# One block for the output product and two feed-forwards, a late norm root, and tensors on 128-byte lines

## The chip, the cores and the metric

One Trainium2 chip, one core. The time is device microseconds (us) of one execution. Engines: PE (TensorE: the matmuls), PEld (its weight loads), DVE (VectorE), ACT (ScalarE), POOL (GpSimd), SP (SyncE, here only the issuer of DMAs).

## The reference, cut to what matters

Two transformer blocks over 512 tokens of width 1024, in float32. The change touches the end of the first and the start of the second:

```
x = x + merged @ w_out                                   # output product
h = rms_norm(x, norm_ffn_g);   g, u = split(h @ w_ffn_in)   # 1024 -> 2 x 2816
x = x + (silu(g) * u) @ w_ffn_out                        # first feed-forward, 2816 -> 1024
h = rms_norm(x, ffn1_pre_g);   g, u = split(h @ ffn1_w_gu)
y = (silu(g) * u) @ ffn1_w_down                          # second feed-forward
x = x + 0.5 * rms_norm(y, ffn1_post_g)                   # post norm
rms_norm(x, g) = x * rsqrt(mean(x * x) + eps) * g
```

The factor rsqrt(...) belongs to a token, so it can be applied before the product with the weights or after it. The rest (attention branches, a state-space branch, a third feed-forward) is not edited.

## The kernel before

Features lie on the 128 partitions, tokens along the free dimension: x is 8 chunks of [128, 512]. Every product is one stream of weight units. A unit holds up to 8 chunks of 128x128 weights (512 KB), loaded by SP into one of two raw slots; ACT rounds it to w_hi (split_hi, line 155), DVE takes w_lo = w_raw - w_hi (split_lo, line 166). Both start when PE has used the unit two places earlier. The moving operand is held as hi and lo too, and each chunk is three matmuls of 512 columns: hi*hi, hi*lo, lo*hi (lines 193 to 195). A tile of 8 chunks is 24 matmuls into one of two banks, acc[0] and acc[1]. The stream runs on through the stages: the last two units of a stage fetch and split the first two of the next.

Each stage is a block of its own: five instruction streams, joined at its end. Four of them matter here.

- `down_stage` for the output product: 8 tiles over `merged`. After each tile DVE adds acc to x (line 649), ACT squares x (line 629), DVE adds that to the sum of squares ssq (line 656).
- `feed_forward_stage`, twice. It opens with `Norm`: PE multiplies ssq by ones (line 326), which gives every partition the sum; ACT takes Ln and Exp of it (lines 336, 338) for rstd; then for each of 8 chunks DVE forms normed = x * gain * rstd (line 357), ACT rounds it to h_hi (line 343), and h_lo = normed - h_hi goes to POOL for even chunks and DVE for odd ones (line 347). Then 22 rounds of a gate tile and an up tile: ACT takes Silu of acc[0], DVE multiplies by acc[1] (line 538), hid is split. Then 8 down tiles of 22 chunks (units of 8, 8 and 6).
- `post_norm_stage` after the second: the same sum over ones, from ssq.

The order of work is the order written in each engine's stream; semaphores hold the counts.

Where the tensors lie. The compiled program of before starts each tensor at the next multiple of 32 bytes in its partition. The shared ones come first: x_res at 16,512 bytes (129 x 128), h_hi at 32,896 (257 x 128), then h_lo, ssq, w_raw, w_hi, w_lo, small (283 columns, 1,132 bytes), ones, ident at 93,952 (734 x 128), all on multiples of 128. Then eps, subln_eps and log_half take one column, that is 32 bytes, each. So whatever a stage allocates starts at 94,560, 96 bytes past a multiple of 128; as their sizes are multiples of 128, hid_hi, hid_lo, merged, y_gla, y_swa, y_da, y_ssd_s, y_xa and mem_h all sit 96 bytes off.

Of the kernel before, what the change touches and what calls it, by code (L numbers as in the profile page):

```python
# [19 lines left out]
F32 = mybir.dt.float32  # L20
F32R = mybir.dt.float32r
# [20 lines left out]
NT = S // P  # L42
MASKED = -1e30
NUM_SEMAPHORES = 256

def small_layout():

    cols, at = {}, 0  # L50
    for name, n in (
        ("norm_mix_g", KC), ("norm_ffn_g", KC), ("ffn1_pre_g_2", KC), ("ffn1_post_g_2", KC),
        ("mix_pre_g_2", KC), ("mix_post_g_2", KC), ("xa_pre_g_2", KC), ("xa_post_g_2", KC),
        ("mem_norm_g_2", KC), ("ffn2_pre_g_2", KC), ("ffn2_post_g_2", KC),
        ("gla_gate_bias_fwd", 4), ("gla_gate_bias_bwd", 4), ("gla_out_norm_g", 2),
        ("swa_q_norm_g", 1), ("swa_k_norm_g", 1), ("b_gate_2", 2 * KC), ("da_subln_g_2", 1),
        ("ssd_conv_w_2", 4 * 24), ("ssd_conv_b_2", 24), ("ssd_norm_g_2", 16),
        ("swa_sinks", 8), ("ssd_D_2", 16), ("ssd_dt_bias_2", 1), ("ssd_A_log_2", 1),
        ("lam_q1", 1), ("lam_k1", 1), ("lam_q2", 1), ("lam_k2", 1),
    ):  # L60
        cols[name] = (at, n)
        at += n
    return cols, at


SMALL, SMALL_N = small_layout()
# [6 lines left out]
def alloc(nc, ctx, c):  # L73

    def sb(name, shape, dt=F32):
        return ctx.enter_context(nc.sbuf_tensor(name, shape, dt))

    c.x = sb("x_res", [P, KC, S])
    c.h_hi = sb("h_hi", [P, KC, S], F32R)
    c.h_lo = sb("h_lo", [P, KC, S], F32R)  # L80
    c.ssq = sb("ssq", [P, S])
    c.raw = sb("w_raw", [P, 2, KC * P])
    c.w_hi = sb("w_hi", [P, 2, KC * P], F32R)
    c.w_lo = sb("w_lo", [P, 2, KC * P], F32R)
# [226 lines left out]
class Norm:  # L311
# [54 lines left out]
    def ready(self, pe, k):  # L366

        pe.wait_ge(self.lo_done[k % 2], k // 2 + 1)
# [90 lines left out]
def feed_forward_stage(c, s_up, s_down, following, gain, in_bank, parts, y, add):  # L459
# [106 lines left out]
    enter(down)  # L566
    c.unit += s_down.rounds * s_down.n
    c.tile += s_down.rounds * s_down.tiles


@stage
# [1705 lines left out]
def build_program(nc, a, out):  # L2277
# [214 lines left out]
```

## Time and profile before

| what | value |
|---|---|
| median of 3 runs | 2982.87 us (2980.98 to 2983.17) |
| profiled execution, first to last instruction (span) | 2979.1 us |
| PE busy | 2715.2 us, 91% of the span |
| DVE, ACT, POOL busy | 42%, 35%, 5% |
| granted TensorE clock, mean | 0.954 |
| output product, the two feed-forwards and their norms | 584.7 to 1387.4 us of the span |

The median lies 3.8 us over the span; the profile has no other time of its own. PE is the busiest engine. The groups further down say where it stands still.

### The profile page before, as it was taken

The numbers are of one execution on the slowest core, as the hardware profiler recorded it, in microseconds if no ns is written. First come the engines' busy times: TensorE is split into PE (matmuls) and PEld (weight loads), VectorE is DVE, ScalarE is ACT, GpSimd is POOL, SyncE is SP. The second block draws the span as 40 slices with busy tenths as digits, with TensorE's granted clock in tenths as the row PEclk, the third lists the DMA queues.
The fourth block names the chain that finished last, engine by engine and source line by source line (L and its number), as shares of the span: only waits on it lengthen the run. The fifth ranks groups of instructions, "written<-read, shape, count | busy, mean of one in ns | idle before, by whom it ended". The sixth has DMA issues, their size and how long they took to land. (4 is left out here: it accounts for less than half of the span.)

```text
span 2979.1 us, 34509 instructions
## 1 busy us (share of the span) xinstructions
PE 2715.2 (91%) x12052; PEld 2163.3 (73%) x12052; DVE 1257.7 (42%) x1709; ACT 1051.7 (35%) x1661; POOL 152.5 (5%) x95
## 2 busy tenths in 40 slices
PE   4998999989999899997899799988899798799997
PEld 3876777768888688885667677766677587588885
DVE  5343543343333433334334235666633633533333
ACT  4443544232222332223344334444422433333221
POOL 0000000000000000001000000111201400100000
PEclk8999999999999999998889899999999899899998
DMA  2121111222223222232111123232222131122332
GB/s 88 64 70 67 64 63 64 85 77 98 99 91 95 78 95 99 94 93 71 45 51 53 53 78 110 97 99 92 71 87 96 64 105 66 55 94 99 99 90 79
DMA packets 69448, 240.86 MB, mean 81 GB/s; under 512 B 7968, under 2 KB 8992, under 8 KB 69264
## 3 DMA queue, kind: packets, MB, share of 16 engines
q1 hardware_dynamic: 69392, 240.14, 24.4%
q8 instruction: 32, 0.52, 0.1%
q14 instruction: 24, 0.20, 0.0%
HBM read 237.94 MB, written 2.16 MB: 81 GB/s over the span
## 5 line engine op out<-in xcount | busy, mean ns | idle before, releaser
L166 DVE TENSOR_TENSOR w_lo<-w_raw,w_hi 128x1024 fp32r<-128x1024 f32 (+1 forms) x422 | 514.1, 1219 | 1081.8 <-ACT w_hi L155 1081.0
L193 PE MATMUL acc<-h_hi,w_hi 128*128 128x512 f32 x2176 | 876.1, 403 | 58.8 <-POOL h_lo L347 19.1
L194 PE MATMUL acc<-h_lo,w_hi 128*128 128x512 f32 x2176 | 856.1, 393 | 0.0
L195 PE MATMUL acc<-h_hi,w_lo 128*128 128x512 f32 x2176 | 856.0, 393 | 0.0
L155 ACT ACTIVATE w_hi<-w_raw 128x1024 fp32r<-128x1024 f32 (+1 forms) x422 | 441.4, 1046 | 1108.4 <-PE acc L195 1106.0
L193 PEld LDWEIGHTS acc<-h_hi,w_hi 128*128 128x128 f32 x2176 | 414.2, 190 | 164.3 <-issue 69.7
L194 PEld LDWEIGHTS acc<-h_lo,w_hi 128*128 128x128 f32 x2176 | 414.5, 190 | 89.9 <-issue 6.1
L195 PEld LDWEIGHTS acc<-h_hi,w_lo 128*128 128x128 f32 x2176 | 413.8, 190 | 88.9
L193 PE MATMUL acc<-10_hid_hi,w_hi 128*128 128x512 f32 x176 | 69.6, 396 | 0.0
L193 PE MATMUL acc<-12_hid_hi,w_hi 128*128 128x512 f32 x176 | 69.6, 396 | 0.0
L193 PE MATMUL acc<-32_hid_hi,w_hi 128*128 128x512 f32 x176 | 69.6, 396 | 0.0
L194 PE MATMUL acc<-10_hid_lo,w_hi 128*128 128x512 f32 x176 | 69.6, 396 | 0.0
L195 PE MATMUL acc<-10_hid_hi,w_lo 128*128 128x512 f32 x176 | 69.6, 396 | 0.0
L194 PE MATMUL acc<-12_hid_lo,w_hi 128*128 128x512 f32 x176 | 69.6, 396 | 0.0
L195 PE MATMUL acc<-12_hid_hi,w_lo 128*128 128x512 f32 x176 | 69.6, 396 | 0.0
L194 PE MATMUL acc<-32_hid_lo,w_hi 128*128 128x512 f32 x176 | 69.6, 396 | 0.0
L195 PE MATMUL acc<-32_hid_hi,w_lo 128*128 128x512 f32 x176 | 69.6, 396 | 0.0
L193 PE MATMUL acc<-merged_hi,w_hi 128*128 128x512 f32 x128 | 52.3, 409 | 12.1 <-PEq L227 6.3
L1067 DVE CUSTOM_DVE_ANT_0 16_s<-16_score,15_mask 128x128 f32<-128x128 f32 (+3 forms) x64 | 29.2, 489 | 62.2 <-PE 16_score L1053 62.2
L2184 DVE SCALAR_TENSOR_TENSOR 20_m<-20_conv_in,20_taps,20_m 128x512 f32<-128x512 f32 x72 | 54.1, 752 | 2.6
L193 PE MATMUL acc<-y_ssd_s_hi,w_hi 128*128 128x512 f32 x128 | 51.4, 402 | 3.5 <-DVE w_lo L166 3.5
L2270 POOL TENSOR_TENSOR 20_xs<-20_xs,20_moved 128x384 f32<-128x384 f32 x16 | 18.5, 1158 | 682.2 <-DVE 20_xs L2253 681.7
(441 smaller groups left out, 3548.9 us busy)
## 6 DMA issues: line engine op xcount, KB each, us to landing
w_raw<-in_w_gu SPq DMA_DIRECT2D x132, 512.0 KB, 3.2
w_raw<-in_w_down SPq DMA_DIRECT2D x48, 512.0 KB, 3.5
w_raw<-in_w_ssd SPq DMA_DIRECT2D x40, 512.0 KB, 3.2
w_raw<-in_w_swa SPq DMA_DIRECT2D x28, 512.0 KB, 3.2
w_raw<-in_w_gla SPq DMA_DIRECT2D x24, 512.0 KB, 3.3
w_raw<-in_w_da SPq DMA_DIRECT2D x24, 512.0 KB, 3.2
w_raw<-in_w_ssd_out SPq DMA_DIRECT2D x24, 512.0 KB, 3.2
w_raw<-in_w_xa SPq DMA_DIRECT2D x24, 512.0 KB, 3.2
```

Source lines behind the costliest of these rows:

```text
L155: c.nc.scalar.activation(c.w_hi[:, k % 2, 0:chunks * P], c.raw[:, k % 2, 0:chunks * P], ACT.Copy).then_inc(c.hi_done, 1)
L166: c.nc.vector.tensor_tensor(c.w_lo[:, k % 2, 0:chunks * P], c.raw[:, k % 2, 0:chunks * P], c.w_hi[:, k % 2, 0:chunks * P].bitcast(F32), AL ...
L193: pe.matmul(out, hi, x_hi[:, j, 0:cols], start=first, stop=False)
L194: pe.matmul(out, hi, x_lo[:, j, 0:cols], start=False, stop=False)
L195: mm = pe.matmul(out, lo, x_hi[:, j, 0:cols], start=False, stop=final)
L1067: dve.tensor_tensor_reduce(to, self.score[j % 2][:, 0:count], self.bias(n), self.scale, floor, ALU.add, ALU.max, self.top[:, par, j:j + 1] ...
L2184: ins = dve.scalar_tensor_tensor(out, u[:, n % 2, k:k + S], tap(k), out, ALU.mult, ALU.add)
L2270: pool.tensor_tensor(y[:, j, P:], y[:, j, P:], moved[:, j % 2, P:], ALU.add).then_inc(q["joined"], 1)
```

## The change

1. `trunk_stage` replaces `down_stage` (output product) and both `feed_forward_stage` calls by one block, so nothing joins the engines between them. The rounds of the output and down products are written out; those of gate and up stay a loop (its first round's PE work is written out).
2. `LateRoot` replaces `Norm`. When a chunk of x is done, ACT writes h_hi = x * gain and DVE h_lo = x * gain - h_hi at once, without the root. PE multiplies ssq by ones after the first gate tile, into a bank of its own; ACT takes the root then, with the same Ln and Exp. DVE multiplies each gate and each up tile by rstd as it leaves acc.
3. ssq is summed by POOL (`gather`), no longer by DVE, from two buffers of squares.
4. `small` is padded to 288 columns, and the three constants share one tensor of 32 columns (128 bytes), so everything allocated after them starts on a multiple of 128.
5. `merged` is read in the new block after its allocation has been closed; hid_lo, written only after the output product, takes its place.

The diff, cut:

```diff
+LINE = 32
...
-    return cols, at
+    return cols, -(-at // LINE) * LINE
...
-    c.eps = sb("eps", [P, 1])
-    c.subln_eps = sb("subln_eps", [P, 1])
-    c.log_half = sb("log_half", [P, 1])
+    constants = sb("constants", [P, LINE])
+    c.eps, c.subln_eps, c.log_half = (constants[:, n:n + 1] for n in range(3))
...
+class LateRoot:
...
+    def split_hi(self, act, t, n, gain):
+        act.wait_ge(self.x_done, n + t + 1)
+        act.activation(self.c.h_hi[:, t, :], self.c.x[:, t, :], ACT.Copy,
+                       scale=self.gain(gain, t)).then_inc(self.hi_done, 1)
...
+    def split_lo(self, dve, t, n, gain):
+        dve.wait_ge(self.hi_done, n + t + 1)
+        at = t
+        dve.scalar_tensor_tensor(self.c.h_lo[:, at, :], self.c.x[:, at, :], self.gain(gain, t),
+                                 self.c.h_hi[:, at, :].bitcast(F32), ALU.mult, ALU.subtract).then_inc(self.lo_done, 1)
+
+    def gather(self, pool, t, par, n):
+        pool.wait_ge(self.squared, n + t + 1)
+        pool.wait_ge(self.summed, (n // KC + 1) + n + t)
+        pool.tensor_tensor(self.c.ssq[:], self.c.ssq[:], self.sq[:, par, :], ALU.add).then_inc(self.summed, 1)
+
+    def mean_square(self, pe, norm):
+        pe.wait_ge(self.summed, (norm + 1) * (KC + 1))
+        pe.matmul(self.mean[:], self.c.ones[:], self.c.ssq[:], start=True, stop=True).then_inc(self.total, 1)
+
+    def root(self, act, norm):
+        act.preload_act_table_set(EXP_LN_SET)
+        act.wait_ge(self.total, norm + 1)
+        act.activation(self.rstd[:], self.mean[:], ACT.Ln, scale=1.0 / D, bias=self.c.eps[:, 0:1]).then_inc(self.log_done, 1)
+        act.wait_ge(self.log_done, norm + 1)
+        act.activation(self.rstd[:], self.rstd[:], ACT.Exp, scale=-0.5).then_inc(self.rstd_done, 1)
...
+        @block.tensor
...
+            for i in range(KC // 2):
+                out_pair(i)
+            for f in range(2):
+                enter(up_phases[f])
+                multiply_tile(c, pe, 0, 0, 0, h, norm=Ready(root.lo_done, KC * f))
+                root.mean_square(pe, f)
+                multiply_tile(c, pe, 0, 1, 1, h)
+                with pe.Fori(1, FFC) as i:
+                    gate_up(i)
+                enter(down_phases[f])
+                for i in range(KC // 2):
+                    down_pair(i, f)
...
+        @block.scalar
+        def _(act):
+            def pair(i, n, units, gain, y):
+                for t in range(2):
+                    for k in range(t * units, (t + 1) * units):
+                        split_hi(c, act, i, k)
+                    if gain is not None:
+                        root.split_hi(act, 2 * i + t, KC * n, gain)
+                    root.square(act, y, 2 * i + t, t, KC * n)
+
+            def gate_up(i, f):
+                split_hi(c, act, i, 0)
+                act.wait_ge(gate_done, FFC * f + i + 1)
+                act.activation(silu[:], gate[:], ACT.Silu).then_inc(silu_done, 1)
+                split_hi(c, act, i, 1)
+                act.wait_ge(hid_done, FFC * f + i + 1)
+                act.activation(hid_hi[:, bass.ds(i, 1), :], hid[:], ACT.Copy).then_inc(hid_hi_done, 1)
...
+                root.root(act, f)
+                act.preload_act_table(ACT.Silu)
+                with act.Fori(0, FFC) as i:
+                    gate_up(i, f)
...
+        @block.vector
...
+            def pair(i, n, units, gain, add):
...
+                    wait_tile(c, dve, i, last)
+                    at = 2 * i + t
+                    if add:
+                        dve.tensor_tensor(c.x[:, at, :], c.x[:, at, :], c.acc[t][:], ALU.add).then_inc(c.acc_free[t], 1)
...
+                    wait_evacuated(c, dve, i, t)
+                    dve.sem_inc(root.x_done, 1)
+                    split_lo(c, dve, i, last)
+                    if gain is not None:
+                        root.split_lo(dve, 2 * i + t, KC * n, gain)
+
+            def gate_up(i, f):
+                n = FFC * f + i
+                wait_tile(c, dve, i, 0)
+                dve.tensor_tensor(gate[:], c.acc[0][:], root.rstd[:], ALU.mult).then_inc(gate_done, 1)
+                dve.wait_ge(gate_done, n + 1)
+                dve.sem_inc(c.acc_free[0], 1)
+                split_lo(c, dve, i, 0)
+                wait_tile(c, dve, i, 1)
+                dve.tensor_tensor(up[:], c.acc[1][:], root.rstd[:], ALU.mult).then_inc(c.acc_free[1], 1)
+                dve.wait_ge(silu_done, n + 1)
+                wait_evacuated(c, dve, i, 1)
+                dve.tensor_tensor(hid[:], silu[:], up[:], ALU.mult).then_inc(hid_done, 1)
+                split_lo(c, dve, i, 1)
+                dve.wait_ge(hid_hi_done, n + 1)
+                dve.tensor_tensor(hid_lo[:, bass.ds(i, 1), :], hid[:], hid_hi[:, bass.ds(i, 1), :].bitcast(F32),
+                                  ALU.subtract).then_inc(hid_lo_done, 1)
...
-            down_stage(c, s_out, s_gu1, *merged, [(0, KC)], c.x, True)
-        feed_forward_stage(c, s_gu1, s_dn1, s_gu2, "norm_ffn_g", False, DOWN, c.x, True)
...
-            feed_forward_stage(c, s_gu2, s_dn2, s_da, "ffn1_pre_g_2", False, DOWN, y, False)
+            trunk_stage(c, merged, (s_out, (s_gu1, s_gu2), (s_dn1, s_dn2)), s_da,
+                        ("norm_ffn_g", "ffn1_pre_g_2"), DOWN, y)
```

## Rows read from the trace of the kernel before

**Rows 1.** The page: part 1, and the high-part split of part 5.

```profile
...
PE 2715.2 (91%) x12052; PEld 2163.3 (73%) x12052; DVE 1257.7 (42%) x1709; ACT 1051.7 (35%) x1661; POOL 152.5 (5%) x95
...
L155 ACT ACTIVATE w_hi<-w_raw 128x1024 fp32r<-128x1024 f32 (+1 forms) x422 | 441.4, 1046 | 1108.4 <-PE acc L195 1106.0
```

**Rows 2.** Busy time by stretch (us, PE, PEld, DVE, ACT, POOL, clock, DMA share, GB/s).

```profile
...
631.00:650.00 19.00, 9.82 (x27) 6.25 (x27) 13.86 (x15) 10.62 (x14) 6.82 (x4) 0.73 0.15 55
650.00:884.00 234.00, 234.00 (x1034) 193.74 (x1033) 79.82 (x85) 69.57 (x86) 0.00 (x0) 1.00 0.29 96
884.00:1007.00 123.00, 123.00 (x529) 99.01 (x527) 38.09 (x41) 28.18 (x32) 0.00 (x0) 1.00 0.30 91
1007.00:1027.00 20.00, 10.34 (x28) 5.97 (x27) 13.86 (x15) 10.57 (x14) 6.82 (x4) 0.74 0.14 52
```

**Rows 3.** Timeline of the first seam (start us, us taken, ...).

```profile
...
630.66 0.40 PE L195 MATMUL acc<-merged_hi,w_lo 128*128 128x512 f32 x1
...
633.33 0.68 DVE L656 TENSOR_TENSOR ssq<-ssq,9_sq 128x512 f32<-128x512 f32 x1
...
634.33 1.10 PE L326 MATMUL acc<-ssq,ones 128*128 128x512 f32 x2 [3.27 <-PEq L227]
...
636.31 0.63 ACT L338 ACTIVATE 11_rstd<-11_rstd 128x512 f32<-128x512 f32 x1
...
640.32 0.76 PE L193 MATMUL acc<-h_hi,w_hi 128*128 128x512 f32 x1 [4.89 <-POOL h_lo L347]
...
640.88 0.63 PE L194 MATMUL acc<-h_lo,w_hi 128*128 128x512 f32 x1
...
641.31 0.63 PE L195 MATMUL acc<-h_hi,w_lo 128*128 128x512 f32 x1
...
650.09 0.40 PE L193 MATMUL acc<-h_hi,w_hi 128*128 128x512 f32 x1
```

**Rows 4.** Timeline of the second seam, first to second feed-forward.

```profile
...
1007.00 0.40 PE L195 MATMUL acc<-10_hid_hi,w_lo 128*128 128x512 f32 x1
...
1010.62 1.28 ACT L333 ACT_TABLE_LOAD   x1 [1.56 <-PEq L469]
...
1010.66 1.91 PE L326 MATMUL acc<-ssq,ones 128*128 128x512 f32 x2 [3.27 <-PEq L469]
...
1012.62 0.69 ACT L336 ACTIVATE 13_rstd<-acc,eps 128x512 f32<-128x512 f32 x1 [0.71 <-PE acc L326]
...
1027.11 0.40 PE L193 MATMUL acc<-h_hi,w_hi 128*128 128x512 f32 x1
```

**Rows 5.** Timeline of PE, where h gives way to hid as moving operand.

```profile
...
881.08 0.39 PE L195 MATMUL acc<-h_hi,w_lo 128*128 128x512 f32 x1
...
884.03 0.40 PE L193 MATMUL acc<-10_hid_hi,w_hi 128*128 128x512 f32 x1
...
886.83 0.40 PE L193 MATMUL acc<-10_hid_hi,w_hi 128*128 128x512 f32 x1
```

**Rows 6.** Groups of PE instructions by operand (busy us, mean ns).

```profile
...
L193 PE MATMUL acc<-h_hi,w_hi 128*128 128x512 f32 x2176 | 876.1, 403 | 58.8 <-POOL h_lo L347 19.1 <-PEq L227 19.0 <-PEq L732 13.2
...
L193 PE MATMUL acc<-10_hid_hi,w_hi 128*128 128x512 f32 x176 | 69.6, 396 | 0.0
...
L193 PE MATMUL acc<-merged_hi,w_hi 128*128 128x512 f32 x128 | 52.3, 409 | 12.1 <-PEq L227 6.3 <-DVE merged_lo L387 5.8
...
L193 PE MATMUL acc<-mem_h_hi,w_hi 128*128 128x256 f32 x128 | 39.1, 306 | 9.6 <-DVE w_lo L166 7.3 <-ACT 29_rstd L336 2.3
...
L193 PE MATMUL acc<-y_swa_hi,w_hi 128*128 128x512 f32 x64 | 25.3, 396 | 0.0
```

**Rows 7.** The low-part split among the groups by form, 640 to 1007 us.

```profile
...
L166 DVE TENSOR_TENSOR w_lo<-w_raw,w_hi 128x1024 fp32r<-128x1024 f32 x59 | 72.4, 1227 | 178.5 <-ACT w_hi L155 178.5
```

**Rows 8.** Timeline of the first seam, POOL beside DVE.

```profile
...
638.47 3.39 POOL L347 TENSOR_TENSOR h_lo<-11_normed,h_hi 128x512 fp32r<-128x512 f32 x2 [606.69 <-ACT h_hi L343]
639.09 1.64 DVE L347 TENSOR_TENSOR h_lo<-11_normed,h_hi 128x512 fp32r<-128x512 f32 x1
```

More of the change, by code:

```diff
@@ L568, in feed_forward_stage, with __init__, gain, clear @@
     c.tile += s_down.rounds * s_down.tiles
+class LateRoot:
+    def __init__(self, c, ctx):
+        sb, ps, sem = local(c, ctx)
+        self.c = c
+        self.sq, self.rstd, self.mean = sb("sq", [P, 2, S]), sb("rstd", [P, S]), ps("mean")
+        self.x_done, self.squared, self.summed = sem("x_done"), sem("squared"), sem("summed")
+        self.hi_done, self.lo_done = sem("h_hi"), sem("h_lo")
+        self.total, self.log_done, self.rstd_done = sem("total"), sem("log"), sem("rstd")
+    def gain(self, name, t):
+        return vec(self.c, name, t)
+    def clear(self, dve):
+        dve.memset(self.c.ssq[:], 0.0).then_inc(self.summed, 1)
+    def split_hi(self, act, t, n, gain):
+        act.wait_ge(self.x_done, n + t + 1)
+        act.activation(self.c.h_hi[:, t, :], self.c.x[:, t, :], ACT.Copy,
+                       scale=self.gain(gain, t)).then_inc(self.hi_done, 1)
+    def square(self, act, y, t, par, n):
+        act.wait_ge(self.x_done, n + t + 1)
+        act.wait_ge(self.summed, (n // KC + 1) + n + t - 1)
+        act.activation(self.sq[:, par, :], y[:, t, :], ACT.Square).then_inc(self.squared, 1)
+    def split_lo(self, dve, t, n, gain):
[16 more added lines that the diff above has]
+        act.activation(self.rstd[:], self.rstd[:], ACT.Exp, scale=-0.5).then_inc(self.rstd_done, 1)
@@ new lines, with __init__, ready, trunk_stage @@
+class Ready:
+    def __init__(self, done, first):
+        self.done, self.first = done, first
+    def ready(self, pe, k):
+        pe.wait_ge(self.done, self.first + k + 1)
+def trunk_stage(c, merged, streams, following, gains, parts, y):
+    s_out, ups, downs = streams
+    order = [s_out, ups[0], downs[0], ups[1], downs[1]]
+    phases, unit, tile = [], c.unit, c.tile
+    for n, s in enumerate(order):
+        phases.append((s, order[n + 1] if n + 1 < len(order) else following, unit, tile))
+        unit, tile = unit + s.rounds * s.n, tile + s.rounds * s.tiles
+    out_phase, up_phases, down_phases = phases[0], phases[1::2], phases[2::2]
+    def enter(phase):
+        c.stream, c.following, c.unit, c.tile = phase
+    with ExitStack() as ctx:
+        sb, ps, sem = local(c, ctx)
+        root = LateRoot(c, ctx)
+        gate, silu, up, hid = sb("gate", [P, S]), sb("silu", [P, S]), sb("up", [P, S]), sb("hid", [P, S])
+        hid_hi, hid_lo = sb("hid_hi", [P, FFC, S], F32R), sb("hid_lo", [P, FFC, S], F32R)
+        gate_done, silu_done, up_done, hid_done, hid_hi_done, hid_lo_done = (
+            sem("gate"), sem("silu"), sem("up"), sem("hid"), sem("hid_hi"), sem("hid_lo"))
+        sources = [(hid_hi[:, a:b, :], hid_lo[:, a:b, :]) for a, b in parts]
+        per = len(parts)
+        block = ctx.enter_context(c.nc.Block())
+        @block.sync
+        def _(sp):
+            for phase in phases:
+                enter(phase)
+                stream_loads(c, sp, c.stream, c.following)
+        @block.tensor
+        def _(pe):
+            h = [(c.h_hi, c.h_lo)]
+            def out_pair(i):
+                for t in range(2):
+                    multiply_tile(c, pe, i, t, t, [merged])
+            def gate_up(i):
+                multiply_tile(c, pe, i, 0, 0, h)
+                multiply_tile(c, pe, i, 1, 1, h)
+            def down_pair(i, f):
+                for t in range(2):
+                    multiply_tile(c, pe, i, t * per, t, sources, norm=None if t else Ready(hid_lo_done, FFC * f))
+            enter(out_phase)
+            for i in range(KC // 2):
[13 more added lines that the diff above has]
+            def pair(i, n, units, gain, y):
+                for t in range(2):
+                    for k in range(t * units, (t + 1) * units):
[10 more added lines that the diff above has]
+                act.activation(hid_hi[:, bass.ds(i, 1), :], hid[:], ACT.Copy).then_inc(hid_hi_done, 1)
+            enter(out_phase)
+            for i in range(KC // 2):
+                pair(i, 0, 1, gains[0], c.x)
+            for f in range(2):
+                enter(up_phases[f])
+                root.root(act, f)
+                act.preload_act_table(ACT.Silu)
+                with act.Fori(0, FFC) as i:
+                    gate_up(i, f)
+                enter(down_phases[f])
+                for i in range(KC // 2):
+                    pair(i, f + 1, per, gains[1] if f == 0 else None, c.x if f == 0 else y)
+        @block.vector
+        def _(dve):
+            def pair(i, n, units, gain, add):
+                for t in range(2):
+                    last = (t + 1) * units - 1
+                    for k in range(t * units, last):
+                        split_lo(c, dve, i, k)
+                    wait_tile(c, dve, i, last)
+                    at = 2 * i + t
+                    if add:
+                        dve.tensor_tensor(c.x[:, at, :], c.x[:, at, :], c.acc[t][:], ALU.add).then_inc(c.acc_free[t], 1)
+                    else:
+                        dve.tensor_copy(y[:, at, :], c.acc[t][:]).then_inc(c.acc_free[t], 1)
+                    wait_evacuated(c, dve, i, t)
[19 more added lines that the diff above has]
+                                  ALU.subtract).then_inc(hid_lo_done, 1)
+                dve.wait_ge(hid_lo_done, n + 1)
+            root.clear(dve)
+            enter(out_phase)
+            for i in range(KC // 2):
+                pair(i, 0, 1, gains[0], True)
+            for f in range(2):
+                enter(up_phases[f])
+                dve.wait_ge(root.rstd_done, f + 1)
+                with dve.Fori(0, FFC) as i:
+                    gate_up(i, f)
+                enter(down_phases[f])
+                root.clear(dve)
+                for i in range(KC // 2):
+                    pair(i, f + 1, per, gains[1] if f == 0 else None, f == 0)
+        @block.gpsimd
+        def _(pool):
+            for n in range(3):
+                for i in range(KC // 2):
+                    for t in range(2):
+                        root.gather(pool, 2 * i + t, t, KC * n)
+    enter(phases[-1])
+    c.unit, c.tile = unit, tile
```

## The prediction

> **What bounds the kernel now.** I read the page first: PE is busy 91% of the span, DVE 42%, ACT 35% [rows 1]. So a saving counts only where it shortens PE's own work or a stretch in which PE stands still. The chain of waits on the page starts only at 2961 us, so it says nothing of this place; I cut the time into stretches instead [rows 2]. In the gate and up rounds and in the down tiles PE is busy for the whole stretch (234.00 of 234.00 us, 123.00 of 123.00) at full clock. Between them lie two seams of 19 and 20 us in which PE works some 10 us at a granted clock of 0.73 and 0.74. There are thus two quantities: what a seam costs, and what one matmul costs in a full stretch.
>
> The timeline of a seam [rows 3]. The last matmul of the output product starts at 630.66, so the next could start at 630.9. From then on the engines follow each other: the split of the last weights, x, its square, ssq done at 634.01; the block ends; the sum over ones at 634.33; Ln, Exp to 636.94; normed, h_hi, h_lo of chunk 0; the first gate matmul at 640.32. It runs at the lower of the two clock levels (1.2 GHz: 0.43 us from start to start at 640.88), then waits for later chunks. The second tile starts at 650.09.
>
> The time of a full tile [rows 5]. With h as moving operand, 13 starts lie in 884.03 - 881.08 = 2.95 us, 226.8 ns each; a tile of 24 is 5.44 us. With hid, 12 lie in 886.83 - 884.03 = 2.80 us, 233.3 ns each. Clock, weights, shape and accumulator are the same, and the change comes with the first hid matmul.
>
> **The two seams.** Undisturbed, the second gate-side tile would start at 630.9 + 5.44 = 636.33; it starts at 650.09: the first seam costs 13.8 us. The second: 1007.0 + 0.23 + 5.44 = 1012.67 against 1027.11, 14.4 us [rows 4]. Together 28.2 us. The change should leave of each, counting from the end E of the product before it:
>
> - Chunk 7 of h. ACT: 0.2 us of lag, w_hi 1.05, h_hi 0.63, square 0.63 (with a gain as scale, taken as 0.63; the nearest row with a per-partition operand is 0.69), done at E+2.5 [rows 1, 3, 4]. DVE: w_lo 1.23 behind w_hi, then h_lo 0.7, done at E+3.3 [rows 7]. PE wants chunk 7 as the last of eight, at 21 x 0.2267 = E+4.8; chunks 0 to 6 are a tile older. The weights of the first gate unit are split since the tile before. Stall 0. Against it: POOL now runs gather, 1.70 us [rows 8], at the same moment. In the old seam one DVE subtraction beside POOL takes 1.64 us [rows 8] where a DVE instruction of that shape alone takes 0.68 [rows 3]. If gather starts first, h_lo ends at E+5.0: 0.2 us late. Bounds 0 and 0.3 us.
> - The sum over ones goes between two tiles of PE. It is two instructions, 1.91 us in the second seam and 1.10 in the first [rows 3, 4]. Both spans reach to the modelled end of the second one, which lies behind the start of what follows. I take 0.9 us of PE time (half of 1.91 is 0.95), bounds 0.8 and 1.1. ssq for it is ready: square E+2.5, gather to E+4.3, or E+5.0 if it yields to DVE, before E+5.44.
> - The root. Sum done E+6.5, Ln 0.69, Exp 0.63: rstd at E+7.9 [rows 3, 4]. DVE then empties acc[0] by E+8.6. Behind the root in ACT's stream stand the Silu table, 1.28 us [rows 4], and the w_hi split for the third tile, 1.05: E+10.3; w_lo behind it E+11.6. PE wants these weights at 5.44 + 0.9 + 5.44 = E+11.8, and acc[0] then as well. It fits by 0.2 us: this is the tightest place of the change. I allow 0.2 us of stall, bounds 0 and 1.0.
>
> So a seam keeps 0.9 + 0.1 + 0.2 = 1.2 us (bounds 0.8 and 2.4), both 2.4 us. Since PE has no pause there, I expect no stretch at the lower clock level either. Gain 28.2 - 2.4 = 25.8 us.
>
> Against it stands the end of the block. The post norm still waits for ssq. Now: E, then 3.1 us to the end of the last addition by DVE (as in the first seam: 634.01 - 630.9) [rows 3]. Then: 0.2 + 1.05 + 0.63 + 0.1 + gather 1.70 = 3.7 us. It costs 0.6 us (bounds 0, if little of this shows, and 1.7, a whole gather). **Net for the seams: 25.2 us.**
>
> **Work inside the rounds, costed at nothing.** DVE's round grows by two multiplications (0.7 us each) and ACT's Silu reads SBUF. After an up tile at T: up, hid, w_lo: 0.15 + 0.7 + 0.7 + 1.23 = T+2.8, hid_lo T+3.5; PE wants w_lo at T+5.44. After a gate tile: gate 0.7, then w_lo at T+2.4. The cover is 2.6 us in each tile; a round would have to lose that much before PE saw it. DVE per round is 2 x 1.23 + 4 x 0.7 = 5.3 us of 10.9. In the output and down tiles DVE's queue holds w_lo behind a wait for x, as before, and h_lo replaces the ssq addition at the same length. gather may hold DVE back 1.7 us at 24 places; the shortest tile there leaves about 2 us. SP's queue keeps its order and its waits. Rolled loops leave no gap at their ends in a full stretch [rows 2], so writing them out gains nothing.
>
> **The lines.** The front section gives the addresses: h and ssq lie on multiples of 128 bytes, everything stage-local 96 bytes off. Another local operand, y_swa, of other size and place, has hid's mean of 396 ns [rows 6]; those of h and merged, 403 and 409, hold the slow seams too. If the start is the reason, each gives back 6.7 ns. The counts, times three for the three products [rows 6]: hid 3 stages x 3 x 176 = 1584; merged 384, y_ssd_s as many; y_swa and its three likes (y_gla, y_da, y_xa) 4 x 192 = 768. Sum 3120 x 6.67 ns = 20.8 us. They stand in stretches that PE sets, except perhaps half of y_gla's 1.3 us. mem_h has half the columns: 384 x 3.3 ns = 1.3 us, of which I count half. For the other 2,020 or so PE instructions of local operands (12,052 less 3 x 2,176 on h, 3,120 and 384) [rows 1, 6] the bound is 3.3 ns each, 6.7 us; most are short and sit in chains of ACT and DVE, I take 0.3 us. **Sum 21 us**, bounds 0 and 28.8 us. For DVE and ACT I take nothing: no row of theirs differs by more than 0.01 us between shared and local tiles of one shape that I saw, and they do not set these stretches.
>
> What speaks against this part: the Trainium skill (SBUF — State Buffer, Specifications) gives SBUF lines of 16 bytes. 96 is a multiple of 16, so by that page the operands lie well already and this term is 0; the rows show a step of 6.7 ns at the first hid matmul, but not what makes it.
>
> **Sum.** 25.2 + 21 = 46.2 us off the profiled span of 2979.1: 2932.9. The median stands 3.8 us above the span, so 2936.7 us.
>
> **Rivals.**
>
> - B, the lines do nothing: what makes hid slower is something else (its size, its distance from its partner). For it: no row has a local tensor on a line. Against it: y_swa and hid differ in size and place and share the pace, and h keeps its own in every stretch. Then 2982.9 - 25.2 = 2957.7 us. 10%.
> - C, a seam keeps a stall: the third tile's weights (0.2 us of room) or h_lo come 3 us late, because the two table loads or a wait between ACT and DVE take longer than their rows. 2 x 3.2 = 6.4 us more: 2943 us. Against it: each step is a row of the old seam. 9%.
> - D, slower: the clock falls in a block that never pauses. For it: PE has not been without a seam for more than 357 us here (650.09 to 1007.0); now it is some 770. Against it: both full stretches hold 1.00 to their end [rows 2]. At the lower level a matmul takes 0.43 instead of 0.23 us [rows 3, 5], so 46.2 us are given back after 231 matmuls, about 100 us of block at half clock. If the clock stayed low for the last 400 us, 1,750 matmuls x 0.2 us = 350 us more: about 3290 us. 3%.
> - E, a cost that eats all: within 0.2% of before. 1%, no mechanism that I can name.
>
> **How the numbers follow.** A, as worked out, has 77%. With every bound in its favour it is 28.2 - 1.6 = 26.6 us for the seams and 28.8 for the lines: 2928. With the bounds against it: seams 28.2 - 4.8 - 1.7 = 21.7; lines (1056 + 192) x 6.7 ns = 8.3 us in this block and half of the other 12.5, 14.5: 2947. The range of 2928 to 2951 us takes A and C and leaves B, D and E out. A measurement of this kernel tells 0.2%, 6 us, from no change. Faster: A, B, C, 96%. Same: 1%. Slower: D, 3%.
>
> **What would show it.** PE's timeline at the seams: last product matmul to second tile in 6.6 us, two instructions on ssq between the first two tiles, granted clock 1.00 through both. A hid matmul's mean of 389 or 390 ns in place of 396, and merged, y_da and the third feed-forward likewise outside the block. POOL with 24 additions of 1.7 us. The forecast is wrong if hid keeps 396 ns, if PE waits on w_lo before the third tile, or if the clock in the last third of the block is below 1.00.

## The result, and the profile of the changed kernel

| | time, median (range, runs) | span of the profiled execution |
|---|---|---|
| before | 2982.57 us (2980.98 to 2983.17, 4) | 2979.1 us |
| changed | 2934.26 us (2933.12 to 2936.50, 4) | 2934.5 us |

The ratio is 0.9843, 95% interval 0.9826 to 0.9860: 48.3 us less. The forecast was 2936.7 us. In every execution on record the time is 1.8 to 2.1 us above that execution's own span. A second set of runs of the same kernel gave 2932.92 us (2931.86 to 2935.45, 6 runs), ratio 0.9850 [0.9828, 0.9871].

The page of the changed kernel, first the engines and then four groups. They answer to [rows 1, 6, 8].

```profile
PE 2687.7 (92%) x12052; PEld 2161.0 (74%) x12052; DVE 1291.6 (44%) x1765; ACT 1051.4 (36%) x1661; POOL 180.4 (6%) x111
...
L193 PE MATMUL acc<-h_hi,w_hi 128*128 128x512 f32 x2176 | 873.8, 402 | 47.7 <-PEq L227 18.5
...
L193 PE MATMUL acc<-9_hid_hi,w_hi 128*128 128x512 f32 x352 | 136.9, 389 | 0.0
...
L613 POOL TENSOR_TENSOR ssq<-ssq,10_sq 128x512 f32<-128x512 f32 x24 | 42.4, 1766 | 1275.7 <-ACT 10_sq L602 1275.7
...
L751 DVE TENSOR_TENSOR 9_gate<-acc,10_rstd 128x512 f32<-128x512 f32 x44 | 30.4, 691 | 105.8 <-PE acc L195 96.0
```

The number of PE instructions is the same. A hid matmul has a mean of 389 ns where it had 396; y_swa, y_da and the hid of the third feed-forward have 389 too. The mean of merged, 407 ns, still holds matmuls at the lower clock level. POOL has 24 additions of 1.77 us; DVE has the 0.69 us multiplications. DVE's added work doesn't show in PE's.

Busy time by stretch, with the columns of [rows 2]: the end of the output product, the first seam with the first gate and up round, the other rounds, the first down stage, the second seam, the second gate and up rounds, the second down stage.

```profile
595.00:626.00 31.00, 31.00 (x138) 25.70 (x137) 16.93 (x17) 11.99 (x17) 9.99 (x6) 1.00 0.31 99
626.00:645.00 19.00, 19.00 (x83) 15.37 (x82) 8.45 (x11) 10.60 (x13) 1.85 (x1) 1.00 0.28 89
645.00:866.00 221.00, 221.00 (x976) 183.00 (x976) 101.79 (x121) 65.84 (x81) 0.00 (x0) 1.00 0.29 96
866.00:986.00 120.00, 120.00 (x531) 99.34 (x531) 40.23 (x42) 32.33 (x39) 12.42 (x7) 1.00 0.32 95
986.00:1004.00 18.00, 18.00 (x79) 14.56 (x78) 8.00 (x10) 9.66 (x12) 1.85 (x1) 1.00 0.34 115
1004.00:1226.00 222.00, 222.00 (x981) 183.87 (x980) 102.25 (x122) 66.76 (x82) 0.00 (x0) 1.00 0.30 96
1226.00:1346.00 120.00, 120.00 (x531) 99.32 (x529) 34.51 (x35) 28.02 (x32) 12.62 (x7) 1.00 0.32 95
```

PE is busy for the whole of each stretch and the granted clock is 1.00, the 2.4 GHz level, also in the stretches that hold the seams. In [rows 2] a stretch of 19 us around the seam had 9.82 us of PE at 0.73.

The timeline of the first seam, beside which [rows 3] are to be laid:

```profile
626.03 0.39 PE L195 MATMUL acc<-merged_hi,w_lo 128*128 128x512 f32 x1
...
626.26 0.39 PE L193 MATMUL acc<-h_hi,w_hi 128*128 128x512 f32 x1
...
626.46 1.06 ACT L155 ACTIVATE w_hi<-w_raw 128x1024 fp32r<-128x1024 f32 x1 [3.25 <-PE acc L195]
626.46 0.69 DVE L739 TENSOR_TENSOR x_res<-x_res,acc 128x512 f32<-128x512 f32 x1 [1.33 <-PE acc L195]
...
627.42 0.70 ACT L595 ACTIVATE h_hi<-x_res,small 128x512 fp32r<-128x512 f32 x1
627.55 1.23 DVE L166 TENSOR_TENSOR w_lo<-w_raw,w_hi 128x1024 fp32r<-128x1024 f32 x1 [0.41 <-ACT w_hi L155]
...
628.69 0.74 DVE L607 SCALAR_TENSOR_TENSOR h_lo<-x_res,small,h_hi 128x512 fp32r<-128x512 f32 x1
628.73 1.85 POOL L613 TENSOR_TENSOR ssq<-ssq,10_sq 128x512 f32<-128x512 f32 x1 [4.15 <-ACT 10_sq L602]
...
631.70 1.02 PE L617 MATMUL 10_mean<-ssq,ones 128*128 128x512 f32 x2
...
632.16 0.80 PE L193 MATMUL acc<-h_hi,w_hi 128*128 128x512 f32 x1
...
632.76 0.69 ACT L622 ACTIVATE 10_rstd<-10_mean,constants 128x512 f32<-128x512 f32 x1 [2.81 <-PE 10_mean L617]
632.80 0.39 PE L194 MATMUL acc<-h_lo,w_hi 128*128 128x512 f32 x1
...
635.43 1.06 ACT L155 ACTIVATE w_hi<-w_raw 128x1024 fp32r<-128x1024 f32 x1
...
636.52 1.22 DVE L166 TENSOR_TENSOR w_lo<-w_raw,w_hi 128x1024 fp32r<-128x1024 f32 x1 [1.50 <-ACT w_hi L155]
...
638.04 0.39 PE L193 MATMUL acc<-h_hi,w_hi 128*128 128x512 f32 x1
```

The first gate matmul follows the last output matmul after 0.23 us, the ordinary distance. h_lo of chunk 7 is done at 629.43, E+3.2 with E = 626.26, long before PE wants it. The addition by POOL starts 0.04 us after h_lo and doesn't hold it back (h_lo takes 0.74 us, the addition 1.85). Between the tiles stands the sum over ones. The root follows; the third tile's low-part weights are done at 637.74 and its first matmul starts at 638.04. Two tiles of 5.44 us and the seam take 638.04 - 626.26 = 11.78 us: **the seam keeps 0.9 us.** The second seam is the same, 986.20 to 997.98.

The same timeline where h gives way to hid, as in [rows 5]:

```profile
863.80 0.39 PE L193 MATMUL acc<-h_hi,w_hi 128*128 128x512 f32 x1
...
866.52 0.39 PE L193 MATMUL acc<-9_hid_hi,w_hi 128*128 128x512 f32 x1
...
869.24 0.39 PE L193 MATMUL acc<-9_hid_hi,w_hi 128*128 128x512 f32 x1
```

12 starts on each side, 2.72 us on each side: 226.7 ns for both. hid had 233.3 before.

The end of the block:

```profile
1345.91 0.39 PE L195 MATMUL acc<-9_hid_hi,w_lo 128*128 128x512 f32 x1
1346.34 1.06 ACT L155 ACTIVATE w_hi<-w_raw 128x1024 fp32r<-128x1024 f32 x1 [3.02 <-PE acc L195]
...
1347.30 0.61 ACT L602 ACTIVATE 10_sq<-y_ffn 128x512 f32<-128x512 f32 x1
...
1347.99 1.78 POOL L613 TENSOR_TENSOR ssq<-ssq,10_sq 128x512 f32<-128x512 f32 x1 [13.15 <-ACT 10_sq L602]
...
1350.12 2.05 PE L905 MATMUL 11_mean<-ssq,ones 128*128 128x512 f32 x2 [3.83 <-PEq L651]
```

Here PE does wait, 3.83 us, for POOL's addition and the end of the block. The same two instructions on ssq took 1.10 us before, at the upper clock level:

```profile
1387.69 1.10 PE L685 MATMUL 14_mean<-ssq,ones 128*128 128x512 f32 x2 [3.28 <-PEq L469]
```

### The profile page after: what moved, and what is told of

Its sections match the earlier page's. It is cut to its first block and busy times, and to the rows that moved or that the text cites. A ratio compares the mean times of both kernels' runs of the same rounds, so it can differ in the third digit from the quotient of the medians.

```text
span 2934.5 us, 34310 instructions
## 1 busy us (share of the span) xinstructions
PE 2687.7 (92%) x12052; PEld 2161.0 (74%) x12052; DVE 1291.6 (44%) x1765; ACT 1051.4 (36%) x1661; POOL 180.4 (6%) x111
## 3 DMA queue, kind: packets, MB, share of 16 engines
q1 hardware_dynamic: 69392, 240.14, 25.2%
## 5 line engine op out<-in xcount | busy, mean ns | idle before, releaser
L193 PE MATMUL acc<-9_hid_hi,w_hi 128*128 128x512 f32 x352 | 136.9, 389 | 0.0
L194 PE MATMUL acc<-9_hid_lo,w_hi 128*128 128x512 f32 x352 | 136.9, 389 | 0.0
L195 PE MATMUL acc<-9_hid_hi,w_lo 128*128 128x512 f32 x352 | 136.9, 389 | 0.0
L613 POOL TENSOR_TENSOR ssq<-ssq,10_sq 128x512 f32<-128x512 f32 x24 | 42.4, 1766 | 1275.7 <-ACT 10_sq L602 1275.7
L194 PEld LDWEIGHTS acc<-9_hid_lo,w_hi 128*128 128x128 f32 x352 | 66.1, 188 | 13.8
L195 PEld LDWEIGHTS acc<-9_hid_hi,w_lo 128*128 128x128 f32 x352 | 66.1, 188 | 13.7
L193 PEld LDWEIGHTS acc<-9_hid_hi,w_hi 128*128 128x128 f32 x352 | 66.1, 188 | 13.7
L193 PE MATMUL acc<-29_hid_hi,w_hi 128*128 128x512 f32 x176 | 68.5, 389 | 0.0
L194 PE MATMUL acc<-29_hid_lo,w_hi 128*128 128x512 f32 x176 | 68.5, 389 | 0.0
L195 PE MATMUL acc<-29_hid_hi,w_lo 128*128 128x512 f32 x176 | 68.5, 389 | 0.0
```

Of the source, the lines that this page charges most:

```text
L193: pe.matmul(out, hi, x_hi[:, j, 0:cols], start=first, stop=False)
L194: pe.matmul(out, hi, x_lo[:, j, 0:cols], start=False, stop=False)
L195: mm = pe.matmul(out, lo, x_hi[:, j, 0:cols], start=False, stop=final)
L613: pool.tensor_tensor(self.c.ssq[:], self.c.ssq[:], self.sq[:, par, :], ALU.add).then_inc(self.summed, 1)
```

## The experiments

Stage lengths in this part run from the start of a stage's first matmul of w_hi to that of the next, from the timelines. No kernel leaves out or changes part of the computation, except that the roots are applied at the place each edit says.

**1 and 2. Each half alone.** `lines_only` is the kernel before with the padding edits (`LINE`, `small_layout`, `constants`); `block_only` is the changed kernel without them:

```diff
-    return cols, -(-at // LINE) * LINE
+    return cols, at
...
-    constants = sb("constants", [P, LINE])
-    c.eps, c.subln_eps, c.log_half = (constants[:, n:n + 1] for n in range(3))
+    c.eps = sb("eps", [P, 1])
+    c.subln_eps = sb("subln_eps", [P, 1])
+    c.log_half = sb("log_half", [P, 1])
```

> The kernel before with nothing changed but small padded to 288 columns and the three constants in one tensor of 128 bytes, so that stage-local tensors start on multiples of 128 bytes. If the start of the moving operand sets the pace: hid, merged and y matmuls take 389 ns in place of 396 (226.7 ns from start to start in place of 233.3) and the kernel 17 to 21 us less than before, about 2963 us. If something else made hid slow (its size or place): no change within 3 us, 2982 us, and the gain of the full change came from the block alone.

> The changed kernel with three separate constants and small unpadded: local tensors again 96 bytes past a line, the block and the late root kept. If the two parts add up: 25 to 26 us less than before, about 2957 us, hid at 396 ns, and with the lines-only kernel's gain the sum is the full gain of 48 us within 2 us. If the parts share their gain (for instance the lines only pay where the block keeps PE full), the two gains sum to clearly less than 48.

Measured: `lines_only` 2960.32 us, ratio 0.9915 [0.9882, 0.9948], span 2960.3. `block_only` 2945.42 us (2936.75 to 2951.99), ratio 0.9886 [0.9859, 0.9913], span 2940.7. The stages:

| us | before | lines_only | block_only | changed |
|---|---|---|---|---|
| output product | 55.59 | 55.58 | 46.44 | 45.54 |
| first gate and up | 243.71 | 243.69 | 240.26 | 240.26 |
| first down | 133.31 | 129.10 | 123.20 | 119.68 |
| second gate and up | 243.71 | 243.70 | 240.28 | 240.26 |
| second down, post norm | 158.94 | 155.96 | 159.48 | 156.81 |
| sum | 835.26 | 828.03 | 809.66 | 802.55 |
| attention's projections and rounds | 272.33 | 271.80 | 261.07 | 272.16 |

The block takes 835.26 - 809.66 = 25.6 us off (forecast 25.2), the lines 7.1 or 7.2 us with or without it (forecast 8.3). By stage the two add up. The medians alone would not say so: by them the block gives some 35 us, not 25. The span of `block_only` looks 11 us too good because of the last row of the table, a stretch with no edit in it. The windows of that stretch, `block_only` and then the changed kernel:

```profile
1392.80:1653.90 261.10, 232.62 (x1018) 175.81 (x1018) 99.70 (x258) 109.81 (x250) 0.00 (x0) 0.90 0.15 51
```

```profile
1383.30:1655.40 272.10, 242.80 (x1017) 185.82 (x1017) 99.27 (x258) 109.81 (x250) 0.00 (x0) 0.86 0.15 49
```

DVE and ACT do the same; PE is at a granted clock of 0.90 in one and 0.86 in the other. It pauses in each of the attention rounds there, and in one of these executions it was longer at the upper level than in the other. The times of some kernels spread likewise (two of the six of `lines_only` are 2941.5 and 2941.7 us, the other four 2959.6 to 2962.7; 6 of the 52 executions of the kernel before lie between 2962.8 and 2969.6, the others at 2978.7 or more), so the verdicts on the two halves are read by stage.

**3 and 4. Local tensors 32 or 64 bytes off.** The edit is a pad behind `constants` (8 columns; 16 for 64 bytes), to find the step at which the pace changes:

```diff
+    sb("pad", [P, 8])
```

> The changed kernel with 32 unused bytes after the constants: local tensors start 32 bytes past a multiple of 128. If any start off a line of 64 or 128 bytes costs the same 6.7 ns: 2955 us, 20 us slower than the changed kernel, hid at 233.3 ns from start to start. If only 96 bytes of offset cost that: less, down to 2934 us.

> The changed kernel with 64 unused bytes after the constants: local tensors start 64 bytes past a multiple of 128. If the line that counts is 128 bytes: as slow as with 32 or 96 bytes, 2955 us, hid at 233.3 ns from start to start. If it is 64 bytes: no change from the changed kernel, 2934 us, 226.7 ns.

Measured: 2947.18 us, ratio 0.9886 [0.9854, 0.9918], and 2945.88 us, ratio 0.9889 [0.9859, 0.9918]. The first down stage is 123.20 us at 32 bytes, as at 96, and 120.87 us at 64. Both medians stand below the 2955 us expected. At 32 bytes the attention stretch is again short, 263.99 us; without that stretch the profiled execution is 18.6 us above the changed kernel's, near the 20 expected. At 64 bytes neither 2955 nor 2934 came out, but a time between them. The groups on hid, at 32 and at 64 bytes:

```profile
L194 PE MATMUL acc<-9_hid_hi,w_hi 128*128 128x512 f32 x352 | 139.1, 395 | 0.0
```

```profile
L194 PE MATMUL acc<-9_hid_hi,w_hi 128*128 128x512 f32 x352 | 138.7, 394 | 0.0
```

So moving the local tensors alone changes the pace, and 64 bytes off costs about a third as much as 32 or 96. The Trainium skill (SBUF — State Buffer, Specifications) gives lines of 16 bytes and a penalty for each cross to a new line. 32, 64 and 96 are all multiples of 16, so nothing on lines there tells these kernels apart; the measured stages do, by 1.2 to 3.5 us. That it is no cost of the start itself comes out in experiments 10 to 12.

**5. The changed kernel again**, as the yardstick of the next ones and to see its spread.

> The changed kernel once more, beside the others of this call, to see how its time spreads. In the profiles so far the stage of the differential attention takes 272 us or 261 to 264 us, by the granted clock in its rounds, whatever the kernel. If that is chance of each execution: most times near 2934 us and some 10 us less. If the changed kernel's own place in time decides it: one value, within 0.2%.

Measured: 2932.92 us, as given above: one value, within 0.12%. The ten executions of this kernel lie between 2931.9 and 2936.5 us, and none is some 10 us below. Ten are too few to say whether the swing in the attention stretch is chance of each execution or belongs to a kernel's own place in time.

**6. The last sum of squares by DVE.**

```diff
                     if gain is not None:
                         root.split_lo(dve, 2 * i + t, KC * n, gain)
+                    else:
+                        root.gather(dve, 2 * i + t, t, KC * n)
...
-            for n in range(3):
+            for n in range(2):
```

> The changed kernel, but the squares of the last product (the second feed-forward's) are summed by DVE again, behind its split, in place of POOL. If POOL's addition of 1.8 us is what made the end of the block later: from the last matmul to the sum over ones 3.4 us in place of 4.0, the kernel 0.5 to 1.4 us faster (the larger figure if the sum over ones then still meets the full clock, 1.1 us in place of 2.05). If the end waits for something else: no change.

Measured: 2935.20 us (2922.71 to 2937.03), ratio 0.9847 [0.9822, 0.9872]. In the trace the wait before the sum over ones falls from 3.83 to 3.28 us and the stage from 156.81 to 156.27:

```profile
1350.16 0.68 DVE L613 TENSOR_TENSOR ssq<-ssq,10_sq 128x512 f32<-128x512 f32 x1
...
1351.17 2.05 PE L907 MATMUL 11_mean<-ssq,ones 128*128 128x512 f32 x2 [3.28 <-PEq L651]
```

Half a microsecond, which the time can't show.

**7. The sum over ones ahead of the first gate tile** instead of behind it: what the order is worth.

```diff
-                multiply_tile(c, pe, 0, 0, 0, h, norm=Ready(root.lo_done, KC * f))
                 root.mean_square(pe, f)
+                multiply_tile(c, pe, 0, 0, 0, h, norm=Ready(root.lo_done, KC * f))
```

> The changed kernel with the sum over ones ahead of the first gate tile in place of behind it; the block, the late scaling and the early h stay. If the gain of a seam needs the first gate tile as cover for the last square and its addition: PE stands 4.3 us at each seam, 8.7 us in all, and 2 to 6 us more if the granted clock falls, so 2943 to 2949 us. If dropping the join of the engines was enough: no change, 2934 us.

Measured: 2947.60 us (2946.25 to 2950.02), ratio 0.9899 [0.9871, 0.9928].

```profile
629.39 1.83 POOL L613 TENSOR_TENSOR ssq<-ssq,10_sq 128x512 f32<-128x512 f32 x1 [3.58 <-ACT 10_sq L602]
...
631.27 2.08 PE L617 MATMUL 10_mean<-ssq,ones 128*128 128x512 f32 x2 [4.18 <-POOL ssq L613]
...
632.36 1.42 PE L193 MATMUL acc<-h_hi,w_hi 128*128 128x512 f32 x1
...
634.42 0.63 PE L193 MATMUL acc<-h_hi,w_hi 128*128 128x512 f32 x1
```

The time is within the range expected (2943 to 2949). PE stands for 4.18 us, the sum takes 2.08 in place of 1.02, and the matmuls after it take 0.63 us until 636.7: the lower clock level, after a pause of 4 us. The stretch from the output product to the second gate rounds is 12.2 us longer for the two seams: 7.8 us of it are the waits (4.18 and, in the second seam, 3.62), and the slower matmuls make most of the rest. So dropping the join of the engines is not enough: the seam's gain needs the first gate tile as cover.

**8. Only h off its place.** h_hi and h_lo start 96 bytes past a multiple of 128; all else stays.

```diff
+    sb("pad_before", [P, 24])
     c.h_hi = sb("h_hi", [P, KC, S], F32R)
     c.h_lo = sb("h_lo", [P, KC, S], F32R)
+    sb("pad_after", [P, 8])
```

> The changed kernel with h_hi and h_lo alone moved to 96 bytes past a line (96 unused bytes ahead of them, 32 behind). If the start of the moving operand alone sets the pace: the 6528 matmuls on h take 233.3 ns in place of 226.7, a gate-and-up stage of 1056 matmuls 247.3 us in place of 240.3, the kernel up to 43 us slower, 2977 us, and hid stays at 226.7. If h was fast for another reason (its place near the weights, its size): the stage stays at 240.3 us.

Measured: 2970.48 us, ratio 0.9975 [0.9958, 0.9993]. Gate and up stages are 247.25 us instead of 240.26; the first down stage keeps its 119.70. So it is not h against hid: the operand that was moved pays.

**9. The third feed-forward likewise** (with the edit of 6): h from x times the gain as each chunk comes, Ln and Exp of the mean square after chunk 3, the root times gate and up as they leave the accumulators.

```diff
+class LateNorm:
...
+    def on_scalar(self, act):
+        for k in range(KC):
+            if k == 4:
+                act.preload_act_table_set(EXP_LN_SET)
+                act.activation(self.rstd[:], self.c.acc[1][:], ACT.Ln, scale=1.0 / D, bias=self.c.eps[:, 0:1]).then_inc(self.log_done, 1)
...
+            act.activation(self.c.h_hi[:, k, :], self.c.x[:, k, :], ACT.Copy,
+                           scale=vec(self.c, self.gain, k)).then_inc(self.hi_done, 1)
...
+                dve.tensor_tensor(gate[:], c.acc[0][:], norm.rstd[:], ALU.mult).then_inc(gate_done, 1)
...
+                dve.tensor_tensor(up_out[:], c.acc[1][:], norm.rstd[:], ALU.mult).then_inc(c.acc_free[1], 1)
```

> The changed kernel with the last product's squares summed by DVE, and with the same late root in the third feed-forward, which keeps its own block: h_hi = x * gain on ACT and h_lo on DVE from the block's first moment, Ln and Exp between the fourth and fifth chunk, gate and up scaled as they leave the accumulators. In the changed kernel this block's second tile starts 15.8 us after its first table load (2544.7 to 2560.5). If the late root pays without the join being dropped: PE starts its first tile 1.5 us into the block, runs it mostly at the lower clock level, and the second tile starts 9 to 10 us in: 6 us less, with the end of the trunk 0.5 us less, about 2927 us. If the gain of the two seams came only from dropping the join, here it stays: 2933 us.

Measured: **2928.68 us** (2925.23 to 2930.44, 5 runs), ratio 0.9820 [0.9807, 0.9834], span 2927.0. The start of that feed-forward, then the same place in the changed kernel:

```profile
2543.49 2.56 ACT L585 ACTIVATE h_hi<-x_res,small 128x512 fp32r<-128x512 f32 x4 [1.48 <-PEq L1036]
...
2545.14 0.47 PE L193 MATMUL acc<-h_hi,w_hi 128*128 128x512 f32 x1 [1.96 <-DVE h_lo L591]
...
2553.05 0.39 PE L193 MATMUL acc<-h_hi,w_hi 128*128 128x512 f32 x1
```

```profile
2544.71 1.28 ACT L333 ACT_TABLE_LOAD   x1 [1.47 <-PEq L885]
...
2550.74 0.76 PE L193 MATMUL acc<-h_hi,w_hi 128*128 128x512 f32 x1 [6.32 <-POOL h_lo L347]
...
2560.51 0.39 PE L193 MATMUL acc<-h_hi,w_hi 128*128 128x512 f32 x1
```

From ACT's first instruction to the second tile: 9.6 us in place of 15.8. This feed-forward still has a block of its own, so the late root gains 6.2 us without the join being dropped. This kernel's median is 4.2 to 5.6 us below those of the changed kernel's two sets; it is the lowest median here.

**10. Only the weights off their place.** The same pads around `c.w_hi` and `c.w_lo`, which start 96 bytes past a multiple of 128; h and all local tensors lie on multiples.

> The changed kernel with w_hi and w_lo, the weights that PE loads, moved to 96 bytes past a line, all moving operands on lines. If a weight load pays for its start as a moving operand does: it takes longer than 190 ns, but lies beside the matmul before it, so a gate-and-up stage of 1056 matmuls stays at 240.3 us, or takes up to 242 us if a quarter of the moving operand's 6.7 ns shows. If it is the bound of the pair: 247 us, as with h moved.

Measured: 2993.21 us (2988.60 to 2996.31), ratio 1.0038 [1.0023, 1.0053]: the changed kernel is slower than before with this one move. Down stage 123.20 us, gate and up 248.24, a little over the 247 expected if the weights bound the pair. Yet the weight loads of hid take the 188 ns that they took; the spacing of the matmuls grew.

```profile
L195 PEld LDWEIGHTS acc<-9_hid_hi,w_hi 128*128 128x128 f32 x352 | 66.0, 188 | 16.2
```

**11. Everything off its place:** one pad of 24 columns ahead of `x_res`, so that x, h, the weights and all locals start 96 bytes past a multiple.

> The changed kernel with 96 unused bytes ahead of x_res, so that every tensor, moving operands and weights alike, starts 96 bytes past a line. Weights off alone made a gate-and-up stage 248.2 us and h off alone 247.3, against 240.3 with both on lines. If the two costs add: 255 us, 241 to 242 ns from start to start, and the kernel some 100 us slower than the changed one. If one of them hides the other: 247 to 249 us, and the kernel near 2993 us.

Measured: 2933.10 us (2932.53 to 2933.68), ratio 0.9854 [0.9768, 0.9941]: nothing lost against the changed kernel, where the expectation had 2993 us or more. The interval is wide, with two executions; the stages decide. Gate and up 240.26, down 119.68 us, the lengths of the changed kernel. The explanation that I held up to here falls: no start is slow by itself.

**12. Weights and locals off, h not:** the pad of 24 columns ahead of `c.w_hi` and none behind `c.w_lo`.

> The changed kernel with 96 bytes put ahead of w_hi alone: w_hi, w_lo, the small shared tensors and every local one start 96 bytes past a multiple of 128, while x, h_hi, h_lo, ssq and w_raw stay on multiples. Moving operands: hid, merged and the y tensors now stand as the weights do, h does not. Theory R (a matmul is slow when its moving operand and its weights start at different places within 128 bytes): the first down stage keeps 119.7 us and hid 226.7 ns from start to start, while a gate and up stage takes 248.2 us as with the weights alone moved; the other products on local tensors keep the pace of the changed kernel. Over the program some 6,530 matmuls on h lose about 8 us in each of three stages, 24 us: median about 2957 us, 2952 to 2972 with what the other matmuls of h in projections add. Theory S (what counts is each operand's own distance from a multiple of 128, and having everything displaced happens to cost nothing because x or w_raw moved with it): hid goes to 233.3 or 235 ns as well, first down stage 123.2 us or more, median about 2990 us.

Measured: 2976.01 us (2973.51 to 2977.68), ratio 0.9978 [0.9964, 0.9991]. The PE groups of 10 and then of 12:

```profile
L195 PE MATMUL acc<-h_hi,w_hi 128*128 128x512 f32 x2176 | 888.1, 408 | 46.1 <-PEq L229 18.5 <-PEq L954 13.3 <-POOL h_lo L349 8.0
L195 PE MATMUL acc<-9_hid_hi,w_hi 128*128 128x512 f32 x352 | 139.1, 395 | 0.0
```

```profile
L194 PE MATMUL acc<-h_hi,w_hi 128*128 128x512 f32 x2176 | 887.4, 408 | 45.8 <-PEq L228 18.5 <-PEq L953 13.0 <-POOL h_lo L348 8.0
L194 PE MATMUL acc<-9_hid_hi,w_hi 128*128 128x512 f32 x352 | 137.1, 389 | 0.0
```

The weights stand at 96 in both. hid at 0 takes 395 ns, hid at 96 takes 389. The stage runs from 881.36 to 1001.04, 119.68 us. With the changed kernel and the rest, by place within 128 bytes:

| weights at | h at | gate and up, us | hid at | first down, us | kernel |
|---|---|---|---|---|---|
| 0 | 0 | 240.26 | 0 | 119.68 | changed |
| 0 | 0 | 240.26 | 96 | 123.20 | block_only |
| 0 | 0 | 240.30 | 32 | 123.20 | off32 |
| 0 | 0 | 240.28 | 64 | 120.87 | off64 |
| 0 | 96 | 247.25 | 0 | 119.70 | h_off |
| 96 | 0 | 248.24 | 0 | 123.20 | w_off |
| 96 | 0 | 248.24 | 96 | 119.68 | w_locals_off |
| 96 | 96 | 240.26 | 96 | 119.68 | all_off |

Every fast entry has moving operand and weights at the same place, every slow one has them apart.

Is the period 128 bytes? By the addresses of the front section and the pads, no run has the two 128 bytes apart: in every fast entry the distance is a multiple of 256 as well. Counted over 256 bytes, from the weights to the moving operand, the distance is -32 for hid in `block_only` and h in `h_off`, +32 for hid in `off32` and `w_off`, +64 for hid in `off64`, and -96 for h in `w_off` and `w_locals_off`. The spacing of successive starts in the traces falls into these same classes: at -32 it alternates between 231 or 232 and 235 ns, at +32 it repeats some 234, 234, 231, 235 (mean 233.3), at -96 it has 237 and 238 ns among them (mean 234.3). Counted over 128 bytes, h in `w_off` would stand as hid does there, and their spacings differ. That speaks for 256 bytes. A run with the two 128 apart, which would settle it, is missing.

Of the last expectation, theory R (the two starts against each other) is borne out; its total of 2957 was too low, because the expectation priced the 3 x 1,056 matmuls of the gate and up stages alone (8.0 us a stage, as measured) and let the other 3,360 on h go with an allowance. The span is 38.8 us above the changed kernel's, 24 of it in these stages.

## Why the prediction was right, point by point

- **What bounds the kernel:** right. PE set every stretch around the change; 34 us more of DVE's work cost nothing [rows 1, 2].
- **The seams, 25.2 us net:** measured 25.6 (`block_only`). Each keeps 0.9 us where 1.2 was forecast. The sum over ones takes 632.80 - 631.70 less one matmul's 0.23, 0.87 us (forecast 0.9). h_lo's 0.1 us of possible delay is 0 (beside the addition it took 1.87 us at three other chunks; at chunk 7 that would end at E+4.3, still before E+4.8), and the third tile's 0.2 is 0: its weights come 0.3 us ahead. That is still the tightest place. No clock was lost; experiment 7, with a pause in each seam, did lose some.
- **The tail, 0.6 us:** the second down stage is 0.5 us longer in `block_only` than before, and 0.85 longer in the changed kernel than in `lines_only`. PE's wait ahead of the sum grew from 3.28 us before to 3.83, and experiment 6, which takes POOL's addition out of the chain, has 3.28 again. So the 0.6 us is right for the wait, 0.55 measured. What it left out is the clock: from the last hid matmul to the next stage the changed kernel takes 37.36 us where the kernel before took 35.97, 1.4 us more, because the sum over ones also takes 2.05 us at the lower level in place of 1.10. In `lines_only` it takes 1.73, in `block_only` 1.16.
- **The lines, 21 us:** about 17 to 19. `lines_only` is 18.8 us below before by its spans, and the changed kernel 17.3 us below `block_only` in all stages but attention's (6.2 by the spans and 11.1 there); the ratio of `lines_only` would allow 15 to 35. The 6.67 ns per matmul is exact: 226.7 from 233.3 ns, and 3.52 us for the 528 matmuls of a down stage. The 8.3 us of this block came out as 7.1: merged gave 0.9 us where 1.3 was counted, and the second down stage gave 2.7 of its 3.5, the rest going to the slower sum over ones. What is short outside the block, up to 3 us, is not traced to a cause.
- **The reason given for the lines:** not the right one. The prediction took the start of a local tensor off a multiple of 128 bytes as the cause. Experiments 10 to 12 show that it is the distance from the place of the weights. The rows of before [rows 5, 6] fit both readings, since in the kernel before the weights lay on a multiple. Padding the local tensors to the weights' place and padding them to a multiple were the same edit, so the size came out nearly right all the same. That was luck: the prediction had no row that told the two readings apart.
- **The sum:** 48.3 us between the medians where 46.2 was forecast, and that closeness is partly luck. The two profiled executions are 2979.1 - 2934.5 = 44.6 us apart, and the parts above come to 43 to 45: the lines gave 2 to 4 us less than forecast. The medians are further apart because the execution profiled before was a quick one of its kernel and the changed kernel's the slowest of its four (2936.50). The 3.8 us that the prediction adds to the span is not a fixed distance either; within one execution it is about 2.0.
- **Rivals:** B (the lines do nothing) is refuted by hid's pace. The 2957.7 us that it gave can be held against `block_only`, which has that case made: 2945.4 us, its profiled execution 11 us shorter in the attention stretch; for its other runs there is no trace to say. C (a stall in a seam) did not happen. D (the clock falls in a block without pauses) did not either: 1.00 to the end, in 720 us from 626 to 1346. What did cost clock was the opposite, a pause.

What stays open: whether the period is 128 or 256 bytes, why 64 bytes apart cost a third of what 32 and 96 do, how weights and moving operand get in each other's way, and what decides in the attention stretch whether the clock stays up.

## What to carry to other kernels

Cut the time of a matmul-bound kernel into stretches and ask of each seam what the matmuls after it truly need; here a scale that is constant over the contraction could wait until the accumulators were emptied, and that gave 25 us in two seams and 6 more in a third. Compare the start-to-start pace of matmuls that differ only in operand: a step of 6.7 ns was worth some 18 us, and a few columns of padding removed it; put moving operand and weights a multiple of 256 bytes apart, as all fast rows here have them. When a tensor's place matters, move each partner by itself and then both together before naming the cause; here a wrong reason stood until the weights had been moved as well, alone and with the others.

## What the runs showed of the hardware that was not expected

- A 128 x 128 by 128 x 512 fp32r matmul in a full stretch starts every 226.7 ns if its moving operand and its weights start at the same place within 128 bytes (a multiple of 256 apart in every such run), and every 233.3 to 234.2 ns if they are 32 or 96 bytes apart (for the upper one, 226.7 ns plus (248.24 - 240.26) / 1,056). 64 apart takes 120.87 us for a stage of 528, 228.9 ns each. The place itself costs nothing (`all_off`, ratio 0.9854, beside 0.9850).
- With the weights moved, the loads of hid's weights still show 188 ns (`w_off`); it is the matmul whose spacing grows.
- h_lo on DVE and the addition on POOL start within 0.04 us of each other 16 times in the changed kernel, and only one of them runs at its short time. 13 times DVE takes 0.74 us and POOL 1.85; at 596.09, 623.29 and 943.79 us DVE takes 1.87 and POOL 1.29.
- A pause of 4.2 us of PE was followed by some 5 us at the 1.2 GHz level (first seam of experiment 7). In the attention stretch, with no edit there, the granted clock was 0.86 in the changed kernel's execution and 0.90 in that of `block_only`, 11 us apart.
